# A 31-tap convolution divided anew between GpSimd, ScalarE and VectorE

## The chip, the cores and the metric

The kernel runs on one core of a Trainium2 chip. The metric is the time on the device in microseconds (us) of one execution; a version is given by the median of several runs, and the profile is one further look at one execution, whose own length is called its span.

## The reference

The program is one mixing block with an MLP and then one attention block with a gated MLP, for one sequence of 256 positions and a width of 2048, all in fp32. Only the front of the first block touches the change:

```python
u = rms_norm(h, mix_pre_gain)
p = einsum("bsd,de->bse", u, w_in)                 # 2048 -> 5120
b_gate, c_gate, v_a, val_b, gate_b = split(p, 5 parts of 1024)
y_a = b_gate * causal_dwconv(c_gate * v_a, conv_a_w)         # 3 taps
g = val_b * sigmoid(gate_b)
g = causal_dwconv(g, conv_b_w) + conv_b_bias                 # 31 taps
y_b = silu(layer_norm(g, ln_b_gain, ln_b_bias))
o = einsum("bse,ed->bsd", concatenate([y_a, y_b]), w_out)
# causal_dwconv: out[t, c] = sum_k w[k, c] * u[t - (K - 1) + k, c]
```

So each of 1024 channels is convolved on its own over the 256 positions, with 31 weights of its own.

## The kernel before, in words

**The weights stream.** Every large product reads its weights in slots of 128x1024 fp32 (512 KB). SyncE loads slot g into a ring of four buffers `raw` as soon as VectorE has finished slot g-4 (`load`, L271 to L277). ScalarE copies it to the rounded `w_hi` (`ticks`, L665 to L676) once the load has landed and TensorE has used slot g-4; VectorE writes the rest, `w_lo = raw - w_hi` (`tick`, L972 to L977). TensorE then runs 12 matmuls on the slot (`slots`, L382 to L403): for each of two k tiles and two token tiles one with `w_lo` (L399) and two with `w_hi` (L400, L401). Eight slots make one unit, a product of 256 tokens with 512 columns. ScalarE and VectorE work four slots (`RING`) ahead of TensorE.

**The units of the input product.** `IN_COLS` (L68) orders ten units, 0 to 9. Units 0 and 1 give the first four channel tiles (of 128 channels) of `g`, units 2 and 3 the other four. After an odd unit u of 1, 3, 5, 7 ScalarE evacuates it (L743), VectorE multiplies value and gate into `zz` (L1081), TensorE transposes `zz` once it has done two slots of the next unit (`in_product`, L449 to L457; `turn`, L405 to L418), and ScalarE copies the transposed tiles to `gT` (after units 1 and 3) or to `cvT` (after 5 and 7) (L749 to L753). Only behind these copies, in ScalarE's program order, stand its next slots. Each of these copies adds one to the semaphore `took`. The input of the 31 taps is `gT`, 8 tiles of 128 channels by 30 + 256 positions.

**The taps.** Tile c of the result is `convb[:, c, :]`, 128x256. Six of the eight tiles are computed on VectorE (`taps_long`, L1023 to L1039): the first tap is a multiplication with the bias added (`tap_first`, L259 to L262), each later one a multiply-and-add into `convb` (L1035), 186 instructions in all. They are a generator, from which VectorE's loop takes three after a slot and four after every fourth (L1061), from unit 2 on; what is left is taken in unit 9 at its sixth slot (L1049 to L1051). Each waits, by the semaphore `conv`, for the instruction on the same tile three earlier. The two tiles of `POOL_TILES`, 3 and 7, are computed by GpSimd (L1409 to L1425): per later tap a product into `prod` (L1419) and an add (L1423), 122 instructions. After that GpSimd computes the 3-tap sums of `y_a` from `cvT`, in two halves of four tiles (L1429 to L1445): 24 multiplications of 128x256 and 4 adds of 128x1024 (L1444). VectorE multiplies them by the gate in `yt` (L1097), after units 8 and 9.

**What follows.** TensorE does slots 0 to 4 of unit 9, waits for all the taps (L471, L472) and forms the mean over channels (L474); VectorE subtracts it (L1045); ScalarE squares (L734); TensorE sums the squares (L481), and so on to `y_b`.

ScalarE's share of the stage is in its loop over units (L727 to L761): the copies to `w_hi`, then the evacuation. It has no part in the taps.

```python
1061                        for _ in range(3 + (s % 4 == 3)):
1062                            next(long_, None)
```

Of the kernel before, what the change touches and what calls it, by code (L numbers as in the profile page):

```python
# [24 lines left out]
P = 128  # L25
# [14 lines left out]
POOL_TILES = (3, 7)  # L40
POOL_STEPS = 2 * K_B - 1
# [34 lines left out]
def build_program(nc, t):  # L76
    ctx = ExitStack()
    with ctx:
# [3 lines left out]
        def at(name, kb, shape, dt=F32):  # L82
            return nc.alloc_sbuf_tensor_at(name, shape, dt, offset=base + int(kb * 1024))
# [4 lines left out]
        def sem(name):  # L88
            return ctx.enter_context(nc.semaphore(name))
# [25 lines left out]
        yb = at("yb", 153.5, [P, CT, S])  # L115
        qkT = at("qkT", 144, [P, 2 * NH, S])
# [73 lines left out]
        conv_pool = sem("conv_pool")  # L190
# [190 lines left out]
        def _(pe):  # L381
# [89 lines left out]
            pe.wait_ge(conv, K_B * (CT - len(POOL_TILES)))  # L471
            pe.wait_ge(conv_pool, POOL_STEPS * len(POOL_TILES))  # L472
# [191 lines left out]
        def _(act):  # L664
# [61 lines left out]

            for u in range(10):  # L727
                if u < 9:
                    ticks(G_IN + u * SPU, RING if u else SPU, RING + SPU)
                else:  # L730
                    ticks(G_IN + u * SPU, RING, RING + 5)
# [239 lines left out]
        def _(dve):  # L971
# [51 lines left out]
            def taps_long():  # L1023
                n = 0
                for half_ in range(2):
                    for k in range(K_B):
                        for c in range(4 * half_, 4 * half_ + 3):
                            if k == 0 and c % 4 == 0:
                                dve.wait_ge(took, 4 * half_ // 2 + 2)
                            if k:  # L1030
                                dve.wait_ge(conv, n - 2)
                            if k == 0:
                                tap_first(nc.vector, c).then_inc(conv, 1)
                            else:
                                nc.vector.scalar_tensor_tensor(convb[:, c, :], gT[:, c, k:k + S],  # L1035
                                                               tap_weight(c, k), convb[:, c, :],
                                                               ALU.mult, ALU.add).then_inc(conv, 1)
                            n += 1
                            yield  # L1039
# [7 lines left out]
            for u in range(10):  # L1047
                for s in range(0 if u else RING, SPU):
# [11 lines left out]
                    if u >= 2:  # L1060
                        for _ in range(3 + (s % 4 == 3)):  # L1061
                            next(long_, None)
# [314 lines left out]
        def _(pool):  # L1377
# [30 lines left out]

            for i, c in enumerate(POOL_TILES):  # L1409
                pool.wait_ge(took, 2 * i + 2)  # L1410
                done = i * POOL_STEPS
                if i:
                    pool.wait_ge(conv_pool, done)
                tap_first(nc.gpsimd, c).then_inc(conv_pool, 1)
                for k in range(1, K_B + 1):
                    if k < K_B:
                        if k > 4:
                            pool.wait_ge(conv_pool, done + 2 * k - 6)
                        nc.gpsimd.tensor_scalar(prod[:, k % 4], gT[:, c, k:k + S], tap_weight(c, k),  # L1419
                                                None, ALU.mult).then_inc(conv_pool, 1)  # L1420
                    if k > 1:
                        pool.wait_ge(conv_pool, done + 2 * k - 2)
                        nc.gpsimd.tensor_tensor(convb[:, c, :], convb[:, c, :],  # L1423
                                                prod[:, (k - 1) % 4], ALU.add
                                                ).then_inc(conv_pool, 1)  # L1425

            pool.wait_ge(line_out, 16 * (SKEWS + 1))
            pool.wait_ge(conv_pool, 2 * POOL_STEPS)
# [96 lines left out]
```

## Time and profile before

| | us |
|---|---|
| median of 3 runs | 2596.45 |
| lowest, highest | 2594.0, 2601.71 |
| span of the profiled execution | 2592.5 |
| TensorE busy in it | 2533.8 |
| VectorE busy | 1472.3 |
| ScalarE busy | 1235.2 |
| GpSimd busy | 245.4 |

The page gives the profiled execution no time besides its span, so the span stands for it; it is 3.95 us under the median. A matmul's recorded busy time overlaps its neighbours', so a busy TensorE is not TensorE at its peak. In the views of the trace L followed by a number is a line of the kernel, "xN" the number of instructions that a row holds, and a duration of merged instructions runs from the start of the first to the end of the last. In a row of the order of time, square brackets hold how long the engine was idle ahead of the row, and what ended that. GpSimd is called POOL, VectorE DVE, ScalarE ACT and TensorE PE. The stage of the change lies between 68 us, when the first `gT` is there, and 272 us, when TensorE begins the mean.

### The profile page before, as it was taken

Reading aid. Unit: us, or ns where it says so; the run is one execution under the profiler, and the core shown is the slowest. Engines: PE = TensorE matmul, PEld = TensorE weight load, DVE = VectorE, ACT = ScalarE, POOL = GpSimd, SP = SyncE. Lnnn points to the kernel's source line nnn. Section 1 sums busy time; section 2 is a strip of 40 time slices with the busy share of each in tenths; the row PEclk is TensorE's granted clock in tenths of the full one; section 3 lists DMA queues with packets and bytes.
Section 4 is the critical chain, followed back from the end, with each engine's and each line's share of the span. In section 5 each row is a group of like instructions: output and inputs, shape, how many; then the busy total and the mean of one; then the engine's idle time right before and its main releaser. Section 6 shows DMA issues by size and latency. Waiting matters only on the chain.

```text
span 2592.5 us, 31914 instructions
## 1 busy us (share of the span) xinstructions
PE 2533.8 (98%) x11389; PEld 2096.6 (81%) x11389; DVE 1472.3 (57%) x1548; ACT 1235.2 (48%) x1509; POOL 245.4 (9%) x199
## 2 busy tenths in 40 slices
PE   8888999999999999989999999999999999999999
PEld 7676778888888888878888888888888888888887
DVE  5899655555545555565566655545545544554554
ACT  5333555444444444454465544444544444444443
POOL 0899200000000000001100000000000000000000
PEclk9999999999999999999999999999999999999999
DMA  7554555565566565545555466665565566565654
GB/s 240 185 153 146 162 171 187 188 194 177 195 189 194 189 190 186 192 145 177 187 188 176 155 203 189 192 194 187 179 195 187 192 193 193 179 198 194 191 188 162
DMA packets 247772, 478.36 MB, mean 185 GB/s; under 512 B 16448, under 2 KB 17016, under 8 KB 247388
## 3 DMA queue, kind: packets, MB, share of 16 engines
q1 hardware_dynamic: 244460, 470.14, 56.8%
q0 software_dynamic: 3152, 6.46, 0.7%
q8 instruction: 85, 1.39, 0.2%
q14 instruction: 43, 0.35, 0.0%
q10 hardware_dynamic: 32, 0.01, 0.0%
HBM read 474.42 MB, written 4.47 MB: 185 GB/s over the span
## 4 chain that ended last, share of the span: by engine, by line
PE 91%; DVE 7%; ACT 1%; DMA 1%; issue 0%; POOL 0%; SPq 0%; ACTq 0%; DVEq 0%
PE acc L399 29%; PE acc L401 29%; PE acc L400 29%; DVE convb L1035 4%; DVE w_lo L976 3%; PE tp L416 2%; DMA raw<-w_in_dram 0%; ACT w_hi L676 0%; PE po L593 0%; DMA h<-x_dram 0%; PE sc L563 0%; DVE h L1147 0%; PE tp L581 0%; PE sc L474 0%; PE po L595 0%
## 5 line engine op out<-in xcount | busy, mean ns | idle before, releaser
L976 DVE TENSOR_TENSOR w_lo<-raw,w_hi 128x1024 fp32r<-128x1024 f32 x888 | 1084.5, 1234 | 927.5 <-ACT w_hi L676 924.0
L676 ACT ACTIVATE w_hi<-raw 128x1024 fp32r<-128x1024 f32 x888 | 930.9, 1060 | 1029.2 <-PE acc L401 960.3
L399 PE MATMUL acc<-w_lo,a_hi 128*128 128x512 f32 x2304 | 910.6, 395 | 11.3 <-DVE w_lo L976 10.6
L400 PE MATMUL acc<-w_hi,a_hi 128*128 128x512 f32 x2304 | 901.1, 391 | 0.0
L401 PE MATMUL acc<-w_hi,a_lo 128*128 128x512 f32 x2304 | 901.1, 391 | 0.0
L399 PEld LDWEIGHTS acc<-w_lo,a_hi 128*128 128x128 f32 x2304 | 435.3, 189 | 109.2 <-DVE w_lo L976 14.7
L401 PEld LDWEIGHTS acc<-w_hi,a_lo 128*128 128x128 f32 x2304 | 434.8, 189 | 91.5
L400 PEld LDWEIGHTS acc<-w_hi,a_hi 128*128 128x128 f32 x2304 | 435.3, 189 | 87.4
L399 PE MATMUL acc<-w_lo,b_hi 128*128 128x512 f32 x1120 | 437.2, 390 | 0.4 <-DVE b_lo L1103 0.4
L401 PE MATMUL acc<-w_hi,b_lo 128*128 128x512 f32 x1120 | 436.3, 390 | 0.0
L400 PE MATMUL acc<-w_hi,b_hi 128*128 128x512 f32 x1120 | 436.3, 390 | 0.0
L399 PEld LDWEIGHTS acc<-w_lo,b_hi 128*128 128x128 f32 x1120 | 210.4, 188 | 44.1 <-DVE b_lo L1103 0.8
L401 PEld LDWEIGHTS acc<-w_hi,b_lo 128*128 128x128 f32 x1120 | 210.4, 188 | 43.5
L400 PEld LDWEIGHTS acc<-w_hi,b_hi 128*128 128x128 f32 x1120 | 210.4, 188 | 43.3
L1391 POOL TENSOR_TENSOR rs<-ms,half 128x2 f32<-128x2 f32 x6 | 4.2, 702 | 1240.2 <-DVE ms L1006 1240.2
L1035 DVE SCALAR_TENSOR_TENSOR convb<-gT,cols,convb 128x256 f32<-128x256 f32 x180 | 114.3, 688 | 0.0
L1419 POOL TENSOR_SCALAR prod<-gT,cols 128x256 f32<-128x256 f32 x60 | 99.4, 1657 | 0.0
L990 DVE TENSOR_TENSOR b_lo<-tp,b_hi 128x512 fp32r<-128x512 f32 x54 | 34.8, 686 | 77.3 <-ACT b_hi L695 77.3
L695 ACT ACTIVATE b_hi<-tp 128x512 fp32r<-128x512 f32 x54 | 29.3, 595 | 98.1 <-PE tp L416 98.1
L686 ACT ACTIVATE ev<-acc,rs 128x512 f32<-128x512 f32 x112 | 69.9, 675 | 0.0
L416 PE MATMUL tp<-ident,zz 128*128 128x128 f32 x344 | 47.4, 283 | 19.6 <-DVE zz L1081 19.6
L416 PEld LDWEIGHTS tp<-ident,zz 128*128 128x128 f32 x344 | 42.0, 146 | 26.1 <-DVE zz L1081 20.8
(155 smaller groups left out, 1007.4 us busy)
## 6 DMA issues: line engine op xcount, KB each, us to landing
raw<-w_in_dram SPq DMA_DIRECT2D x272, 512.0 KB, 3.8
raw<-w_down_dram SPq DMA_DIRECT2D x216, 512.0 KB, 4.7
raw<-w_gu_dram SPq DMA_DIRECT2D x176, 512.0 KB, 4.4
raw<-w_up_dram SPq DMA_DIRECT2D x128, 512.0 KB, 3.7
raw<-w_out_dram SPq DMA_DIRECT2D x64, 512.0 KB, 4.4
raw<-w_branch_dram SPq DMA_DIRECT2D x32, 512.0 KB, 3.6
skew_dram<-line_dram POOLq DMA_DIRECT2D x3, 768.0 KB, 14.1
h<-x_dram SPq DMA_DIRECT2D x4, 512.0 KB, 7.8
```

Of the source, the lines that this page charges most:

```text
L399: nc.tensor.matmul(out, xh, wl, start=s == 0 and k == 0, stop=False)
L400: nc.tensor.matmul(out, xh, wh, start=False, stop=False)
L401: mm = nc.tensor.matmul(out, xl, wh, start=False, stop=s == n - 1 and k == KS - 1)
L416: tr = nc.tensor.transpose(tp[:, g, (2 * k + tk) * P:(2 * k + tk + 1) * P], src[:, tk, c:c + P], ident[:, :])
L676: nc.scalar.activation(w_hi[:, ring], raw[:, ring], ACT.Copy).then_inc(hi_ready, 1)
L686: a_ = nc.scalar.activation(dst[:, tk], acc[:, pair, tk], func, scale=rs[:, n, tk:tk + 1])
L695: nc.scalar.activation(dst[:, bass.ds(k0 + 2 * g, 2), :].rearrange("p k s -> p (k s)"), tp[:, g, :], ACT.Copy).then_inc(split_hi, 1)
L976: nc.vector.tensor_tensor(w_lo[:, ring], raw[:, ring], w_hi[:, ring].bitcast(F32), ALU.subtract).then_inc(lo_ready, 1)
L990: nc.vector.tensor_tensor(lo_, tp[:, g, :], hi_.bitcast(F32), ALU.subtract).then_inc(split_lo, 1)
L1035: nc.vector.scalar_tensor_tensor(convb[:, c, :], gT[:, c, k:k + S], tap_weight(c, k), convb[:, c, :], ALU.mult, ALU.add).then_inc(conv, 1)
L1391: nc.gpsimd.tensor_tensor(rs[:, n, :], ms[:, n, :], half[:, :], ALU.pow).then_inc(rs_ok, 1)
L1419: nc.gpsimd.tensor_scalar(prod[:, k % 4], gT[:, c, k:k + S], tap_weight(c, k), None, ALU.mult).then_inc(conv_pool, 1)
```

## The change

GpSimd takes no part in the 31 taps and goes straight from its transfers to the 3-tap sums. The taps are arranged by tap and half (four tiles) instead of by tile. Of each half the taps k = 0, 3, 6, ... 30 (eleven) stay on VectorE tile by tile, with the instructions of before; for the other twenty ScalarE multiplies `gT` by the weights, four instructions of 128x256 into one of four new buffers `scaled`, and VectorE adds the buffer to the four tiles of `convb` in one instruction of 128x1024. `LONG_OPS` is VectorE's list, 128 instructions; `SCALED` has the 40 (half, tap) pairs of ScalarE, 160 instructions. ScalarE takes three of these after each slot of units 2 to 8 and what is left ahead of unit 9; VectorE takes two of its own after a slot, and three after every fourth. ScalarE waits before a buffer's reuse until VectorE has added its last content; VectorE waits before an add for the buffer (`conv_scaled`) and for its own instruction just before. The four buffers lie in parts of `b_hi` and `b_lo` that are written only later, for `y_b`.

```diff
--- before.py
+++ after.py
@@ -37,8 +37,12 @@
 D_A = D // 2
 K_A, K_B = 3, 31
 CT = D_A // P
-POOL_TILES = (3, 7)
-POOL_STEPS = 2 * K_B - 1
+LONG_OPS = tuple((half, k, q)
+                 for half in range(2) for k in range(K_B)
+                 for q in (range(4) if k % 3 == 0 else (None,)))
+SCALED = tuple((half, k) for half, k, q in LONG_OPS if q is None)
+SCALED_AT = tuple(n for n, op in enumerate(LONG_OPS) if op[2] is None)
+BUFS = 4
 FF1 = 4 * D
 FF2 = 5632
 NH = 16
@@ -113,6 +117,8 @@
         convb = at("convb", 162, [P, CT, S])
         dg = at("dg", 170, [P, TT, P])
         yb = at("yb", 153.5, [P, CT, S])
+        scaled = [at("scaled0", 88, [P, 4, S]), at("scaled1", 92, [P, 4, S]),
+                  at("scaled2", 104, [P, 4, S]), at("scaled3", 108, [P, 4, S])]
         qkT = at("qkT", 144, [P, 2 * NH, S])
         m_hi = at("m_hi", 144, [P, KT, S], F32R)
         m_lo = at("m_lo", 160, [P, KT, S], F32R)
@@ -187,7 +193,7 @@
         h_ready = sem("h_ready")
         step0 = sem("step0")
         conv = sem("conv")
-        conv_pool = sem("conv_pool")
+        conv_scaled = sem("conv_scaled")
         conv3 = sem("conv3")
         ya = sem("ya")
         ln_pe = sem("ln_pe")
@@ -468,8 +474,7 @@
             last_in(0, 2)
             in_product(9)
             last_in(2, 5)
-            pe.wait_ge(conv, K_B * (CT - len(POOL_TILES)))
-            pe.wait_ge(conv_pool, POOL_STEPS * len(POOL_TILES))
+            pe.wait_ge(conv, len(LONG_OPS))
             for c in range(CT):
                 mm = nc.tensor.matmul(sc[:, 0:S], mean_w[:, :], convb[:, c, :], start=c == 0,
                                       stop=c == CT - 1)
@@ -724,10 +729,33 @@
                 squares(0, c, h[:, :, c], 2 * c)
 
 
+            def scale_taps():
+
+                for i, (half_, k) in enumerate(SCALED):
+                    act.wait_ge(took, 2 * half_ + 2)
+                    if i >= BUFS:
+                        act.wait_ge(conv, SCALED_AT[i - BUFS] + 1)
+                    for q in range(4):
+                        c = 4 * half_ + q
+                        a_ = nc.scalar.activation(scaled[i % BUFS][:, q, :], gT[:, c, k:k + S],
+                                                  ACT.Copy, scale=tap_weight(c, k))
+                        if q == 3:
+                            a_.then_inc(conv_scaled, 1)
+                        yield
+
+            taps = scale_taps()
+
             for u in range(10):
-                if u < 9:
+                if u < 2:
                     ticks(G_IN + u * SPU, RING if u else SPU, RING + SPU)
+                elif u < 9:
+                    for s in range(SPU):
+                        ticks(G_IN + u * SPU, RING + s, RING + s + 1)
+                        for _ in range(3):
+                            next(taps, None)
                 else:
+                    for _ in taps:
+                        pass
                     ticks(G_IN + u * SPU, RING, RING + 5)
                     for half_ in range(2):
                         act.wait_ge(ln_dve, half_ + 1)
@@ -1021,22 +1049,27 @@
 
 
             def taps_long():
-                n = 0
-                for half_ in range(2):
-                    for k in range(K_B):
-                        for c in range(4 * half_, 4 * half_ + 3):
-                            if k == 0 and c % 4 == 0:
-                                dve.wait_ge(took, 4 * half_ // 2 + 2)
-                            if k:
-                                dve.wait_ge(conv, n - 2)
-                            if k == 0:
-                                tap_first(nc.vector, c).then_inc(conv, 1)
-                            else:
-                                nc.vector.scalar_tensor_tensor(convb[:, c, :], gT[:, c, k:k + S],
-                                                               tap_weight(c, k), convb[:, c, :],
-                                                               ALU.mult, ALU.add).then_inc(conv, 1)
-                            n += 1
-                            yield
+
+                for n, (half_, k, q) in enumerate(LONG_OPS):
+                    if k == 0 and q == 0:
+                        dve.wait_ge(took, 2 * half_ + 2)
+                    if q is None:
+                        i = SCALED_AT.index(n)
+                        dve.wait_ge(conv, n)
+                        dve.wait_ge(conv_scaled, i + 1)
+                        part = convb[:, 4 * half_:4 * half_ + 4, :]
+                        nc.vector.tensor_tensor(part, part, scaled[i % BUFS][:, :, :], ALU.add
+                                                ).then_inc(conv, 1)
+                    else:
+                        c = 4 * half_ + q
+                        if k == 0:
+                            tap_first(nc.vector, c).then_inc(conv, 1)
+                        else:
+                            dve.wait_ge(conv, n - q)
+                            nc.vector.scalar_tensor_tensor(convb[:, c, :], gT[:, c, k:k + S],
+                                                           tap_weight(c, k), convb[:, c, :],
+                                                           ALU.mult, ALU.add).then_inc(conv, 1)
+                    yield
 
             long_ = taps_long()
 
@@ -1058,7 +1091,7 @@
                                                 ).then_inc(ln_dve, 1)
                     tick(G_IN + u * SPU, RING + s)
                     if u >= 2:
-                        for _ in range(3 + (s % 4 == 3)):
+                        for _ in range(2 + (s % 4 == 3)):
                             next(long_, None)
                 if u == 0:
 
@@ -1406,26 +1439,7 @@
                            ).then_inc(gain1_in, 16)
 
 
-            for i, c in enumerate(POOL_TILES):
-                pool.wait_ge(took, 2 * i + 2)
-                done = i * POOL_STEPS
-                if i:
-                    pool.wait_ge(conv_pool, done)
-                tap_first(nc.gpsimd, c).then_inc(conv_pool, 1)
-                for k in range(1, K_B + 1):
-                    if k < K_B:
-                        if k > 4:
-                            pool.wait_ge(conv_pool, done + 2 * k - 6)
-                        nc.gpsimd.tensor_scalar(prod[:, k % 4], gT[:, c, k:k + S], tap_weight(c, k),
-                                                None, ALU.mult).then_inc(conv_pool, 1)
-                    if k > 1:
-                        pool.wait_ge(conv_pool, done + 2 * k - 2)
-                        nc.gpsimd.tensor_tensor(convb[:, c, :], convb[:, c, :],
-                                                prod[:, (k - 1) % 4], ALU.add
-                                                ).then_inc(conv_pool, 1)
-
             pool.wait_ge(line_out, 16 * (SKEWS + 1))
-            pool.wait_ge(conv_pool, 2 * POOL_STEPS)
             for half_ in range(2):
                 pool.wait_ge(took, 4 + 2 * half_ + 2)
                 sums = conva[:, 4 * half_:4 * half_ + 4, :]
```

## Rows read from the trace of the kernel before

**Rows 1.** Page: busy time by engine; shares of the chain by line

```profile
PE 2533.8 (98%) x11389; PEld 2096.6 (81%) x11389; DVE 1472.3 (57%) x1548; ACT 1235.2 (48%) x1509; POOL 245.4 (9%) x199
PE acc L399 29%; PE acc L401 29%; PE acc L400 29%; DVE convb L1035 4%; DVE w_lo L976 3%; PE tp L416 2%; DMA raw<-w_in_dram 0%; ACT w_hi L676 0%; PE po L593 0%; DMA h<-x_dram 0%; PE sc L563 0%; DVE h L1147 0%; PE tp L581 0%; PE sc L474 0%; PE po L595 0%
```

**Rows 2.** Stretches: busy us (x) PE, PEld, DVE, ACT, POOL; clock; DMA; GB/s

```profile
90.00:120.00 30.00, 21.72 (x89) 15.87 (x87) 29.39 (x40) 9.65 (x10) 30.00 (x24) 0.95 0.54 168
330.00:360.00 30.00, 30.00 (x134) 24.86 (x133) 14.62 (x12) 13.88 (x17) 0.00 (x0) 1.00 0.59 194
```

**Rows 3.** Chain of waits in order of time: start us, us, what

```profile
80.52 11.45 DMA raw<-w_in_dram
...
118.87 1.14 DVE zz L1081
120.06 1.98 PE tp L416 x8
...
174.76 1.15 DVE zz L1081
...
231.69 1.15 DVE zz L1081
...
271.90 3.72 PE sc L474 x16
```

**Rows 4.** Who waited for whom, 92 to 272 us: in total, times, longest

```profile
PE tp L416 <- DVE zz L1081: 19.6, 3, 6.7
PE acc L399 <- DVE w_lo L976: 9.9, 13, 2.9
```

**Rows 5.** VectorE in order of time: start, us, instruction, idle before

```profile
34.12 0.16 DVE L1004 TENSOR_REDUCE ms<-ssq 128x2 f32<-128x8 f32 x1 [3.48 <-ACT junk L709]
34.32 0.17 DVE L1006 TENSOR_SCALAR ms<-ms 128x2 f32<-128x2 f32 x1
...
71.53 1.27 DVE L1035 SCALAR_TENSOR_TENSOR convb<-gT,cols,convb 128x256 f32<-128x256 f32 x3
...
93.09 1.35 DVE L976 TENSOR_TENSOR w_lo<-raw,w_hi 128x1024 fp32r<-128x1024 f32 x1 [0.61 <-ACT w_hi L676]
...
127.82 1.89 DVE L1035 SCALAR_TENSOR_TENSOR convb<-gT,cols,convb 128x256 f32<-128x256 f32 x3
...
236.46 1.42 DVE L976 TENSOR_TENSOR w_lo<-raw,w_hi 128x1024 fp32r<-128x1024 f32 x1 [3.64 <-ACT w_hi L676]
...
249.97 3.41 DVE L976 TENSOR_TENSOR w_lo<-raw,w_hi 128x1024 fp32r<-128x1024 f32 x1
...
258.84 1.71 DVE L1035 SCALAR_TENSOR_TENSOR convb<-gT,cols,convb 128x256 f32<-128x256 f32 x3
...
261.61 2.11 DVE L1035 SCALAR_TENSOR_TENSOR convb<-gT,cols,convb 128x256 f32<-128x256 f32 x4
263.64 1.27 DVE L1097 TENSOR_TENSOR yt<-tp,conva 128x512 f32<-128x512 f32 x2
...
267.05 1.41 DVE L976 TENSOR_TENSOR w_lo<-raw,w_hi 128x1024 fp32r<-128x1024 f32 x1
```

**Rows 6.** VectorE group with the new add's shape, whole run

```profile
L1187 DVE TENSOR_TENSOR wide<-wide,ev 128x1024 f32<-128x1024 f32 x16 | 19.5, 1219 | 0.3 <-ACT ev L683 0.3
```

**Rows 7.** ScalarE in order of time

```profile
122.56 2.00 ACT L676 ACTIVATE w_hi<-raw 128x1024 fp32r<-128x1024 f32 x2
...
131.36 1.06 ACT L676 ACTIVATE w_hi<-raw 128x1024 fp32r<-128x1024 f32 x1 [1.66 <-PE acc L401]
...
140.49 1.25 ACT L686 ACTIVATE ev<-acc,rs 128x512 f32<-128x512 f32 x2
...
298.27 1.09 ACT L768 ACTIVATE yb<-convb,cols 128x256 f32<-128x256 f32 x2
```

**Rows 8.** GpSimd in order of time: the three-tap sums, first and last

```profile
231.57 4.67 POOL L1439 TENSOR_SCALAR conva<-cvT,cols 128x256 f32<-128x256 f32 x4 [0.16 <-issue]
...
272.11 3.09 POOL L1444 TENSOR_TENSOR conva<-conva,prod 128x1024 f32<-128x1024 f32 x1
```

## The prediction

> **What bounds the kernel now.** I read the page first: TensorE is busy for 98% of the span and holds nearly all of the chain that ended last, but VectorE's tap line L1035 has 4% of that chain, some 100 us, and only this stage has those taps [rows 1]. The stretches come next: with its work undisturbed TensorE has 134 matmul records in 30 us, and between 90 and 120 us only 89, while VectorE is busy for 29.4 of 30 [rows 2]. So VectorE bounds the stage. The chain in order of time shows how. It holds one slow load up to 92.0 us, then almost only VectorE up to a product `zz` (ends at 120.0; the first of three here), the transposes, and VectorE again to the second `zz` (ends at 175.9) and the third (232.8), until TensorE starts the mean at 271.9 [rows 3]. TensorE's waits agree: 19.6 us for the three `zz` and 9.9 us for `w_lo` [rows 4].
>
> One round from `zz` to `zz` is 16 slots and took 55.9 and 56.9 us. TensorE's own pace is 2.72 us a slot (1.66 idle + 1.06, where ScalarE follows TensorE [rows 7]), so its round is 43.5 plus 2.0 for the transposes, 45.5.
>
> **The new price of VectorE's work.** A tap took 1.89 us for three, pitch 0.60 once the overlap of 0.08 is taken off, while GpSimd worked on the taps; the same three took 1.27, pitch 0.40, at 71.5 us, before GpSimd had begun [rows 5]. Beside GpSimd's 3-tap sums it is 1.71 for three, pitch 0.54 [rows 5]. The new add has the shape of L1187, 1.219 us, pitch 1.14 [rows 6]. GpSimd's 122 instructions go, and with them the 0.20 a tap. The new list is 88 single taps at 0.40 (35.2) and 40 adds at 1.14 (45.6), 80.8 us. Of these, 40 adds and 20 first-of-four taps wait for the instruction just before. Nearest row: a multiplication that waits for its predecessor starts at 34.32, 0.04 after that one's end at 34.28, where an unwaiting one would start 0.08 before the end [rows 5]; so 0.12 each. A slot's subtraction stands between in almost half the cases, so 35 of them, 4.2 us. Sum 85.0 over 128, or 0.66 each; bounds 0.63 (no such wait) and 0.78 (a tap stays at 0.60).
>
> The Trainium skill, "VectorE: DVE Perf Modes", section "The DRAIN you can't avoid", has the next operation start only when the pipe is empty, semaphore or not, so that these waits would cost nothing. The rows show an overlap of 0.08 that a wait would lose, so here they disagree; by that rule 4.2 us less would be spent in the whole list.
>
> **The sum, stretch by stretch.**
>
> First, up to 92 us the loads govern: one took 11.45 us [rows 3]. GpSimd's transfers that compete with it are not moved, and VectorE had only 0.61 us idle before 93.09 [rows 5]; I take no gain here (bounds 0 and 2).
>
> Second, 93.1 to the first `zz`: 8 subtractions at 1.14 (9.1), 18 list entries at 0.66 (12.0; before, 26), `zz` 1.14: it ends at 115.3 instead of 120.0, gain 4.7.
>
> Third, the round to 175.9: idle after `zz` 3.64, as the row at 236.46 shows for this pattern [rows 5], 16 subtractions 18.2, 36 entries 23.9, `zz` 1.14, together 46.9 against 55.9: gain 9.0. TensorE's 45.5 lies just under it.
>
> Fourth, the round to 232.8. GpSimd now starts the 3-tap sums when the second `zz` has been transposed and copied, not at 231.57 [rows 8], so half of them falls in here. What they cost VectorE: from 236.46 to 263.64 it did 8 subtractions and 26 taps in 27.2 us, which at 1.14 and 0.40 would be 9.1 + 10.4 = 19.5, so 7.7 more: 0.14 on each tap (3.6), and about 4 for subtractions or taps held behind GpSimd's large adds, as the subtraction of 3.41 us at 249.97 beside the usual 1.21 [rows 5]. With 11 taps instead of 26 that is 6.2. The round is 53.1 against 56.9: gain 3.8.
>
> Fifth, unit 8, where the second half of the 3-tap sums runs (from the third `zz` on) as before: 9.1 + 12.0 + 6.2 = 27.3 against 27.2: gain 0.
>
> Sixth, unit 9: `w_lo` for slot 4 is ready at 268.5 [rows 5], TensorE needs 2.72, so 271.2; the mean waited until 271.9 for the last taps [rows 3]. With two entries left instead of four or more, the wait goes: gain 0.7. What is late next is slot 4 itself, behind `yt` and its roundings. GpSimd's last add, which held VectorE up to 277.3 (3.09 us from 272.11 [rows 8]), ends earlier; this lies under TensorE's two slots of 5.4 us, and I give it nothing.
>
> **ScalarE.** The 160 multiplications are hidden only while its round fits. From `zz` to its first copy to `w_hi` 2.55 us (120.01 to 122.56); 16 copies at pitch 0.94 (2.00 for two) 15.2; two evacuations of 1.25, 2.4; `zz` 1.15; and 48 multiplications of x. That is 21.3 + 48x. The price x is not in the trace. The nearest row is a 128x256 activation out of SBUF with a column as scale and one as bias, 1.09 us for two, pitch 0.49 [rows 7]; with one column I take 0.45 (bounds 0.38, under which nothing of this length falls, and 1.06, the whole 128x1024 copy). The round is 42.9, hidden under VectorE's 46.9 by 4 us. By order, the entry that VectorE needs in a slot has been produced in the same slot of ScalarE or earlier, up to three earlier in the second half, and ScalarE's wait for a free buffer is for an entry one to five slots back, so neither waits in steady state. A late ScalarE would hold back `w_hi`, for which VectorE and then TensorE wait. SyncE's loads wait for `w_lo`; at TensorE's pace 194 GB/s flow without a wait [rows 2].
>
> In all 4.7 + 9.0 + 3.8 + 0 + 0.7 = 18.2 us. The sum is made against the span of 2592.5, giving 2574.3; the median shown is 3.95 above that span, and the predicted median is 2596.45 - 18.2 = 2578.2. About 0.3%, 8 us, is what a measurement of this kernel can tell from no change.
>
> **Rivals.**
>
> (a) *TensorE becomes the bound* (0.20). If the 3-tap sums no longer hurt VectorE and its own waits cost nothing, rounds fall to 45.5. Then the gains are 5.3, 10.4, 11.4, and in unit 9 up to 5.7 (eleven slots, 29.9, and transposes, 1.5, after 234.8 make 266.2 instead of 271.9): 32.8, or 2563.7. For it: TensorE's round is only 1.4 us below VectorE's. Against: the 3-tap sums visibly stretch VectorE [rows 5].
>
> (b) *GpSimd holds up the long adds* (0.12). The Trainium skill, "SBUF — State Buffer", section "Who interferes with whom", has VectorE and GpSimd share a port pair as an exclusive lock, held for a whole instruction by whoever starts first, whenever VectorE has two inputs in SBUF and GpSimd reads there. As a mechanism of this kernel: in each of the two halves of the 3-tap sums some 5.6 adds run, and each waits for one GpSimd multiplication of 1.2 us (4.67 us for four [rows 8]). That costs 6.7 twice, 18.2 - 13.4 = 4.8 us gained, 2591.6. Against: subtractions of the same shape were mostly at 1.21 beside GpSimd [rows 5].
>
> (c) *ScalarE becomes the bound, and the kernel is slower* (0.06). It decides at x = 0.53, where 21.3 + 48x reaches 46.9, and makes the round longer than before from x = 0.72. At 0.85, in the upper half of my bounds (each multiplication stopping at its wait for the buffer), the rounds are 62.1, 6.2 and 5.2 longer, the first stretch 2.5 and unit 8 2: 16 slower, 2612. Against: 0.85 is nearly the pitch of a 128x1024 copy, for a quarter of its elements.
>
> (d) *The change doesn't free VectorE*: GpSimd leaves, but a tap stays at 0.60, so something else had stretched it. At 0.78 an entry the rounds are 51.1; gains 2.5, 4.8 and 5.8 (no stretch added), 13 in all; it lies within my range and I count it with the forecast.
>
> **Chances and range.** Forecast (gain 10 to 26) 0.62, (a) 0.20, (b) 0.12, (c) 0.06. Low 2562 takes in (a); high 2592 takes in (b)'s centre and the bad ends of the prices. Faster by over 0.3% is 0.62 less 0.02, plus 0.20, plus a quarter of (b): 0.83. Within 0.3%: 0.11, mostly (b). Slower: 0.06.
>
> **What would show it.** Right: taps at 0.40 pitch up to the second `zz`; adds at 1.22 us; a `zz` round of about 47 us and then 53; multiplications on ScalarE of about 0.5 us; TensorE's wait for `zz` down from 6.5 us to 1 or 2 each; VectorE still leading the chain. Wrong: ScalarE's `w_hi` as releaser of long VectorE idle times ((c)); adds above 1.5 us after 165 us ((b)); TensorE alone in the chain there ((a)); or a first `zz` that does not come earlier than 120 us, which would mean that the loads govern beyond 93 us.

## The result, and the profile after

The changed kernel takes 2575.35 us (median of four runs, 2574.43 to 2577.28) against 2596.93 for the kernel before (now also four runs); the ratio is 0.9914 with a 95% interval of 0.9891 to 0.9937, so 16 to 28 us faster. The span of its profiled execution is 2574.3 us, 18.2 less than the 2592.5 of before.

The page of the changed kernel, engines and shares of the chain by line, beside [rows 1]. L1061 is the new add, L1069 the single tap, L740 the multiplication on ScalarE:

```profile
PE 2531.6 (98%) x11389; PEld 2097.8 (81%) x11389; DVE 1444.6 (56%) x1490; ACT 1296.4 (50%) x1669; POOL 101.9 (4%) x77
...
PE acc L405 30%; PE acc L407 30%; PE acc L406 30%; PE tp L422 2%; DVE w_lo L1004 1%; DVE convb L1061 1%; DVE convb L1069 1%; DMA raw<-w_in_dram 0%; ACT w_hi L681 0%; ACT scaled L740 0%; PE po L598 0%; PE sc L568 0%; DMA h<-x_dram 0%; DVE h L1180 0%; PE tp L586 0%
```

VectorE's taps had 4% of the chain; the two tap lines now have 2% together, and TensorE's three matmul lines have gone from 29% to 30% each. GpSimd's busy time is down by 143 us, ScalarE's up by 61. Two stretches of the changed kernel, to be held against [rows 2]:

```profile
90.00:120.00 30.00, 24.26 (x102) 19.63 (x101) 25.00 (x30) 21.44 (x40) 0.00 (x0) 0.89 0.55 165
120.00:150.00 30.00, 30.00 (x134) 24.83 (x133) 29.53 (x38) 27.07 (x49) 0.00 (x0) 1.00 0.66 193
248.00:252.80 4.80, 4.51 (x13) 3.60 (x14) 4.43 (x6) 1.33 (x2) 0.00 (x0) 0.66 0.50 154
```

TensorE has 102 records between 90 and 120 us where it had 89, and 134, its full number, in the next 30; the third row is read further down. VectorE in order of time, to be held against [rows 3, 5] (start us, us, instruction, idle before):

```profile
73.16 2.48 DVE L1061 TENSOR_TENSOR convb<-convb,scaled 128x1024 f32<-128x1024 f32 x2
...
76.70 1.27 DVE L1069 SCALAR_TENSOR_TENSOR convb<-gT,cols,convb 128x256 f32<-128x256 f32 x3
...
114.33 1.22 DVE L1114 TENSOR_TENSOR zz<-ev 128x1024 f32<-128x1024 f32 x1
119.18 1.23 DVE L1004 TENSOR_TENSOR w_lo<-raw,w_hi 128x1024 fp32r<-128x1024 f32 x1 [3.63 <-ACT w_hi L681]
...
161.18 1.22 DVE L1114 TENSOR_TENSOR zz<-ev 128x1024 f32<-128x1024 f32 x1
...
179.47 2.52 DVE L1069 SCALAR_TENSOR_TENSOR convb<-gT,cols,convb 128x256 f32<-128x256 f32 x1
...
190.40 3.40 DVE L1004 TENSOR_TENSOR w_lo<-raw,w_hi 128x1024 fp32r<-128x1024 f32 x1
...
213.85 1.22 DVE L1114 TENSOR_TENSOR zz<-ev 128x1024 f32<-128x1024 f32 x1
...
243.60 1.28 DVE L1130 TENSOR_TENSOR yt<-tp,conva 128x512 f32<-128x512 f32 x2
```

and the end of the stage in the chain that ended last:

```profile
252.75 3.61 PE sc L479 x16
```

The chain counts the mean from the end of the matmul before it; its first matmul starts at 252.55, 189.1 us after the `zz` that follows unit 1, and this is the figure to which the runs below are held. Three taps in a row took 1.27 us, and two adds 2.48, each 1.23, 0.02 apart. The `zz` start at 114.33, 161.18 and 213.85. GpSimd's 3-tap sums have moved forward, into the third round (from 164.5 us; their second half begins at 217.61). Each of the two long adds there holds up one VectorE instruction: beside the add at 178.89 a single tap takes 2.52 us, beside the one at 190.34 a subtraction takes 3.40:

```profile
164.49 6.29 POOL L1453 TENSOR_SCALAR conva<-cvT,cols 128x256 f32<-128x256 f32 x4 [90.15 <-ACT cvT L779]
...
178.89 2.81 POOL L1458 TENSOR_TENSOR conva<-conva,prod 128x1024 f32<-128x1024 f32 x1
...
190.34 2.38 POOL L1458 TENSOR_TENSOR conva<-conva,prod 128x1024 f32<-128x1024 f32 x1
```

**Where the time went.** All from the start of the `zz` after unit 1, which is at 64.00 before and 63.46 after:

| stretch | before | after | gain | predicted |
|---|---|---|---|---|
| to the first `zz` of the stage | 54.79 | 50.87 | 3.9 | 4.7 |
| second round | 55.90 | 46.85 | 9.1 | 9.0 |
| third round | 56.92 | 52.67 | 4.3 | 3.8 |
| third `zz` to `yt` (unit 8) | 32.03 | 29.75 | 2.3 | 0 |
| `yt` to the mean (unit 9) | 8.26 | 9.15 | -0.9 | 0.7 |
| sum | 207.90 | 189.29 | 18.6 | 18.2 |

**Which engine sets each round.** The second round is no longer VectorE's. TensorE's transposes after the three `zz`, with its idle time before them:

```profile
115.60 1.97 PE L422 MATMUL tp<-ident,zz 128*128 128x128 f32 x8 [5.08 <-DVE zz L1114]
...
162.45 1.09 PE L422 MATMUL tp<-ident,zz 128*128 128x128 f32 x8 [0.22 <-DVE zz L1114]
...
215.12 1.75 PE L422 MATMUL tp<-ident,zz 128*128 128x128 f32 x8 [3.01 <-DVE zz L1114]
```

Between the first two rows TensorE is idle for those 0.22 us and nothing more, so its own work fills the round: 1.6 us until the first matmul of the slots, 16 slots of 2.72 (43.5), and about 1.3 us because the first matmuls run at a low granted clock (0.50 from 114 to 117 us, 0.53 from 117 to 120), start to start 0.43 us instead of 0.23. From 115.6 to 154.2 us the chain that ended last consists of TensorE's matmuls alone. ScalarE waits 0.46 us for TensorE before a copy to `w_hi`, and near the end VectorE waits for that copy:

```profile
154.17 1.06 ACT L681 ACTIVATE w_hi<-raw 128x1024 fp32r<-128x1024 f32 x1 [0.46 <-PE acc L407]
```

```profile
155.26 1.23 DVE L1004 TENSOR_TENSOR w_lo<-raw,w_hi 128x1024 fp32r<-128x1024 f32 x1 [0.85 <-ACT w_hi L681]
```

Without that wait VectorE's round would be about 46.0 us, so the two engines are within 1 us of each other. From 92.6 us to the first `zz`, in the third round and in unit 8 VectorE is behind, as TensorE's waits of 5.08 and 3.01 us show.

### The profile page after: what moved, and what is told of

Same layout as the page of the kernel before. It is cut to its first block, busy times and chain, and to the rows that moved or that the text cites. A ratio compares the mean times of both kernels' runs of the same rounds, so it can differ in the third digit from the quotient of the medians.

```text
span 2574.3 us, 31968 instructions
## 1 busy us (share of the span) xinstructions
PE 2531.6 (98%) x11389; PEld 2097.8 (81%) x11389; DVE 1444.6 (56%) x1490; ACT 1296.4 (50%) x1669; POOL 101.9 (4%) x77
## 4 chain that ended last, share of the span: by engine, by line
PE 93%; DVE 4%; issue 1%; ACT 1%; DMA 1%; POOL 0%; ACTq 0%; SPq 0%; DVEq 0%
PE acc L405 30%; PE acc L407 30%; PE acc L406 30%; PE tp L422 2%; DVE w_lo L1004 1%; DVE convb L1061 1%; DVE convb L1069 1%; DMA raw<-w_in_dram 0%; ACT w_hi L681 0%; ACT scaled L740 0%; PE po L598 0%; PE sc L568 0%; DMA h<-x_dram 0%; DVE h L1180 0%; PE tp L586 0%
## 5 line engine op out<-in xcount | busy, mean ns | idle before, releaser
L740 ACT ACTIVATE scaled<-gT,cols 128x256 f32<-128x256 f32 x160 | 69.5, 497 | 8.3 <-DVE convb L1061 8.3
L688 ACT ACTIVATE ev<-acc 128x1024 f32<-128x1024 f32 x48 | 48.5, 1011 | 13.2 <-PE acc L407 13.2
```

The costliest lines, as they stand in the source:

```text
L688: nc.scalar.activation(dst, acc[:, pair], func).then_inc(evacuated, 1)
L740: a_ = nc.scalar.activation(scaled[i % BUFS][:, q, :], gT[:, c, k:k + S], ACT.Copy, scale=tap_weight(c, k))
```

## The experiments

Each ratio below is against runs of the kernel before on the same chip, whose median was 2595.0 to 2596.0 in these series. It is formed from the runs and not from the two medians, from whose quotient it differs by up to 0.002. The changed kernel was not run again in these series: where a run is set against it by a few us, the two come from different chips, the intervals of the ratios overlap, and the trace has to show the difference.

**One half of the change: GpSimd leaves, VectorE does all.** `all_vector` takes the taps from GpSimd and gives none to ScalarE:

```diff
-                 for q in (range(4) if k % 3 == 0 else (None,)))
+                 for q in range(4))
...
-                        for _ in range(2 + (s % 4 == 3)):
+                        for _ in range(4 + s % 2):
                             next(long_, None)
```

> GpSimd leaves the 31 taps, but ScalarE does not step in: VectorE computes all 248 of them one tile at a time. Theory (a tap costs VectorE 0.40 us once GpSimd is silent, and 0.54 to 0.60 beside it): a round from zz to zz is 3.6 idle + 18.2 subtractions + 72 taps at 0.40 (28.8) + about 1.2 for taps that wait for their predecessor + 1.1 = 53 us, against 55.9 before; the round and the unit with the 3-tap sums are longer than before (about 62 and 33 us). In all some 5 us slower than the kernel before, about 2602 us. Rival (taps stay at 0.60 whatever GpSimd does): a round of 67 us and 2635 us or more. Rival (the long adds are what brings the gain, GpSimd's silence nothing): the same as that.

Measured: 2594.93 us, ratio 0.9994 (0.9981 to 1.0006): no change. VectorE's group of taps from 70 to 265 us, and its `zz` in order of time:

```profile
L1069 DVE SCALAR_TENSOR_TENSOR convb<-gT,cols,convb 128x256 f32<-128x256 f32 x240 | 112.1, 514 | 1.7
```

```profile
118.66 1.22 DVE L1114 TENSOR_TENSOR zz<-ev 128x1024 f32<-128x1024 f32 x1
...
171.53 1.22 DVE L1114 TENSOR_TENSOR zz<-ev 128x1024 f32<-128x1024 f32 x1
...
231.29 1.22 DVE L1114 TENSOR_TENSOR zz<-ev 128x1024 f32<-128x1024 f32 x1
```

The second round is 52.9 us, as expected, with taps of 0.514 against 0.689 in the same stretch of the kernel before. The third is 59.8 instead of 62, so the 3-tap sums cost it 6.9, not 9. So GpSimd's silence pays for the 62 taps that VectorE took over, and for nothing more. The expected loss of 5 us did not come: up to the mean the stage is only 1 us longer than in the kernel before.

**The other half: ScalarE and the grouped adds help, GpSimd stays.** `keep_pool` has the new division for six tiles, and GpSimd's loop of before for the other two:

```diff
-                 for q in (range(4) if k % 3 == 0 else (None,)))
+                 for q in (range(3) if k % 3 == 0 else (None,)))
...
+            for i, c in enumerate(POOL_TILES):
...
-                        part = convb[:, 4 * half_:4 * half_ + 4, :]
+                        part = convb[:, 4 * half_:4 * half_ + 3, :]
```

> ScalarE and the grouped adds help with six tiles (120 multiplications, 40 adds of 128x768), and GpSimd keeps its two tiles as before. Theory: VectorE's list is 66 single taps at 0.60 and 40 adds of about 0.99, 78 us in all against 85 in the changed kernel, so the rounds are about 46 us; but GpSimd ends its taps only at about 227 us, and the first half of the 3-tap sums at about 250, for which yt waits: GpSimd becomes the bound, and the mean starts at about 260 us instead of 252.8. About 2582 us, 7 slower than the changed kernel. Rival (GpSimd beside VectorE costs more than it computes): rounds of 50 us and more, adds above 1.2 us. Rival (keeping GpSimd is free, and only VectorE's list counts): 2572.

Measured: 2598.97 us, ratio 1.0002 (0.9987 to 1.0016): no change either, where a gain was expected. GpSimd's adds and the new adds of VectorE by group (68 to 290 us), and the wait of `yt`:

```profile
L1460 POOL TENSOR_TENSOR convb<-convb,prod 128x256 f32<-128x256 f32 x60 | 67.1, 1119 | 0.2
...
L1065 DVE TENSOR_TENSOR convb<-convb,scaled 128x768 f32<-128x768 f32 x40 | 47.8, 1196 | 3.0 <-ACT scaled L744 2.4
```

```profile
123.05 1.74 DVE L1118 TENSOR_TENSOR zz<-ev 128x1024 f32<-128x1024 f32 x1
...
180.27 1.21 DVE L1118 TENSOR_TENSOR zz<-ev 128x1024 f32<-128x1024 f32 x1
...
233.47 1.21 DVE L1118 TENSOR_TENSOR zz<-ev 128x1024 f32<-128x1024 f32 x1
...
267.00 1.29 DVE L1134 TENSOR_TENSOR yt<-tp,conva 128x512 f32<-128x512 f32 x2 [9.46 <-POOL conva L1481]
```

The rounds are 57.2 and 53.2 us, not 46, as the first rival said. An add of 768 elements takes 1.196 us on average, nearly as long as one of 1024 beside an idle GpSimd (1.223), and GpSimd's own adds have gone from 0.956 to 1.119. The average hides two cases: up to 170 us most of these adds take 1.40 us or more, from 176 to 235 us most take 0.95, though GpSimd works throughout; why was not tried. The theory's other half held too: GpSimd ends its taps at 242.5 us, and `yt` waits 9.5 us for the 3-tap sums. I had priced the long adds at 0.99 beside GpSimd. Each half of the change is worth nothing alone, and both together 21 us.

**GpSimd's old instructions put back, for nothing.** `pool_busy` is the changed kernel with the loop of before on GpSimd, its sum going to a spare tile:

```diff
+            for i, c in enumerate((3, 7)):
+                pool.wait_ge(took, 2 * i + 2)
...
+                        nc.gpsimd.tensor_tensor(spare[:, :], spare[:, :],
+                                                prod[:, (k - 1) % 4], ALU.add
```

> The changed kernel, with GpSimd given its 122 former instructions back, their result going to a spare tile that nobody reads. Theory (GpSimd's instructions stretch VectorE's): single taps go from 0.40 to 0.60 pitch, the second round from 46.9 to 51 or 52 us; the 3-tap sums start only at about 225 us, so yt waits for them up to about 250 us. 2588 us, 13 slower than the changed kernel. Rival (the lock holds every long add for a GpSimd instruction too): adds of 1.8 us or more, a second round of 58 us and 2600 or more. Rival (GpSimd's silence is worth nothing): 2575.

Measured: 2610.22 us, ratio 1.0062 (1.0041 to 1.0084), 35 us over the changed kernel where 13 were expected. VectorE by group in about one round, first in `pool_busy` (125 to 178 us), then in the changed kernel (117 to 162 us):

```profile
L1006 DVE TENSOR_TENSOR w_lo<-raw,w_hi 128x1024 fp32r<-128x1024 f32 x16 | 23.2, 1450 | 3.6 <-ACT w_hi L683 3.6
L1071 DVE SCALAR_TENSOR_TENSOR convb<-gT,cols,convb 128x256 f32<-128x256 f32 x22 | 14.2, 681 | 0.1
L1063 DVE TENSOR_TENSOR convb<-convb,scaled 128x1024 f32<-128x1024 f32 x10 | 13.6, 1356 | 0.2
```

```profile
L1004 DVE TENSOR_TENSOR w_lo<-raw,w_hi 128x1024 fp32r<-128x1024 f32 x16 | 19.6, 1222 | 4.7 <-ACT w_hi L681 4.5
L1061 DVE TENSOR_TENSOR convb<-convb,scaled 128x1024 f32<-128x1024 f32 x10 | 12.2, 1223 | 0.2
L1069 DVE SCALAR_TENSOR_TENSOR convb<-gT,cols,convb 128x256 f32<-128x256 f32 x22 | 9.7, 481 | 0.1
```

The single taps grew by 0.200 us, as the theory said (22 of them, 4.4 us). What it had left out are the subtractions, by 0.228 (16, 3.6 us), and the adds, by 0.133 (10, 1.3 us): the round is 55.5 us instead of 46.85, 8.6 more and not 4.4. The first stretch and the third round are longer by 7.2 and 6.0 us, and the way from the third `zz` to `yt` by 14.3; that holds a wait of 12.15 us for GpSimd, itself late:

```profile
280.07 1.29 DVE L1132 TENSOR_TENSOR yt<-tp,conva 128x512 f32<-128x512 f32 x2 [12.15 <-POOL conva L1482]
```

So both my theory (taps only) and its first rival (every add held, 1.8 us) were off: taps, subtractions and adds, which all read two operands in SBUF, are all stretched, by 0.13 to 0.23 us on average.

**The 3-tap sums left out.** In `no_three` GpSimd fills their tile with ones:

```diff
-                for k in range(K_A):
...
+                for q in range(2 * K_A - 1):
+                    v = nc.gpsimd.memset(sums[:, :, 52 * q:min(52 * q + 52, S)], 1.0)
+                    v.then_inc(conv3, 1)
```

> The changed kernel with GpSimd's 3-tap sums left out (their tile is filled with ones instead, so y_a is not computed). Theory (the 3-tap sums stretch VectorE by about 6 us in each of two stretches): the third round is 47 us instead of 52.7, unit 8 drops from 25.1 to 21 us or less, and TensorE becomes the bound there; the mean starts about 10 us earlier, 2565 us. Rival (they run beside VectorE and cost nothing on the path): 2575.

Measured: 2564.27 us, ratio 0.9882 (0.9864 to 0.9900).

```profile
161.49 1.22 DVE L1114 TENSOR_TENSOR zz<-ev 128x1024 f32<-128x1024 f32 x1
...
208.33 1.22 DVE L1114 TENSOR_TENSOR zz<-ev 128x1024 f32<-128x1024 f32 x1
...
234.68 1.28 DVE L1130 TENSOR_TENSOR yt<-tp,conva 128x512 f32<-128x512 f32 x2
```

The third round is 46.8 us instead of 52.7, and from the third `zz` to `yt` it is 26.4 instead of 29.8. In both stretches VectorE's only idle time, with the sums or without, is the one after `zz`, so the sums cost it 5.8 us in the third round (I had taken 6.2) and 3.4 in unit 8. The difference is in the long adds: of the two in each half one holds up a tap by 2 us in either stretch, and the other a subtraction by 2.2 in the third round only; in unit 8 it starts at 243.54 us, as `yt` begins.

**ScalarE's room.** `double_scale` does each multiplication twice:

```diff
+                        nc.scalar.activation(twin[i % BUFS][:, q, :], gT[:, c, k:k + S],
+                                             ACT.Copy, scale=tap_weight(c, k))
```

> The changed kernel with each of the 160 multiplications done twice on ScalarE (the second into a spare tile). Theory (ScalarE's round is 21.3 + 48x, decides at x = 0.53 and loses against the kernel before from x = 0.72; the twins make x = 0.80): rounds of 60 us, 27 us slower than the changed kernel, 2602 us, and slower than the kernel before. Rival (ScalarE has room beside TensorE's pace): under 2585 us.

Measured: 2608.01 us, ratio 1.0032 (1.0015 to 1.0049), slower than the kernel before, and 33 us over the changed kernel instead of 27.

```profile
123.74 1.22 DVE L1118 TENSOR_TENSOR zz<-ev 128x1024 f32<-128x1024 f32 x1
...
183.49 1.23 DVE L1118 TENSOR_TENSOR zz<-ev 128x1024 f32<-128x1024 f32 x1 [0.27 <-ACT ev L693]
...
243.23 1.23 DVE L1118 TENSOR_TENSOR zz<-ev 128x1024 f32<-128x1024 f32 x1 [0.26 <-ACT ev L693]
```

Rounds of 59.75 and 59.74 us: 21.3 + 48 x 0.80 is 59.7, and the second and third `zz` wait for ScalarE's evacuation. The formula of rival (c) holds; what was not in the expectation are 8.6 us more in the first stretch and 4.3 in unit 8. In the changed kernel three multiplications take 1.29 us, pitch 0.40:

```profile
78.33 1.29 ACT L740 ACTIVATE scaled<-gT,cols 128x256 f32<-128x256 f32 x3
...
196.96 0.51 ACT L740 ACTIVATE scaled<-gT,cols 128x256 f32<-128x256 f32 x1 [4.67 <-DVE convb L1061]
```

so ScalarE's work in a round is 21.3 + 19.2 = 40.5 us there, 6.3 under the round's 46.85. The last row is a wait of 4.67 us for a free buffer, which I had said would not occur in steady state; it begins at 192.3, while VectorE is held behind GpSimd's long add (190.40 to 193.80). `bufs6` asks whether it costs:

```diff
-BUFS = 4
+BUFS = 6
```

> The changed kernel with six buffers scaled instead of four. Theory: ScalarE's 8.3 us of waits for a buffer go, but VectorE was not waiting for what they delayed: 2575 us, within 1 us. Rival (the waits for a buffer in the third round, one of 4.7 us, hold back w_hi): 2 to 4 us faster.

Measured: 2574.99 us, ratio 0.9897 (0.9850 to 0.9943). The interval is too wide to tell 2 to 4 us from none; the trace shows no gain: the mean begins 188.9 us after the `zz` of unit 1, and 189.1 in the changed kernel.

**The idle time after `zz`.** `hoist` moves one of ScalarE's copies to `w_hi` ahead of its copies to `gT` and `cvT`; `hoist2` moves two (`hoist_bufs6` is `hoist` with six buffers):

```diff
-                        ticks(G_IN + u * SPU, RING + s, RING + s + 1)
+                        if s or u % 2:
+                            ticks(G_IN + u * SPU, RING + s, RING + s + 1)
...
                     i = u // 2
...
+                    ticks(G_IN + (u + 1) * SPU, RING, RING + 1)
```

> The changed kernel, with ScalarE copying the next slot to w_hi ahead of its copies to gT and cvT instead of behind them (four times). Theory (VectorE bounds the rounds, and its 3 to 3.6 us of idle time after each zz are on the path): the idle time after zz goes, and each round shortens until TensorE's 45.5 us bind: 1.4 in the second round, 3.6 in the third, about 3 in unit 8. 8 us faster than the changed kernel, 2567 us. Rival (ScalarE or TensorE sets the rounds): 2575. Rival (the copies to gT and cvT come 1 us later and delay the taps and the 3-tap sums): 2576 to 2578.

> The earlier copy to w_hi and six buffers together. Theory: the idle time after zz is what costs, and once it is gone the third round is set by VectorE beside the 3-tap sums: 2567 us, as with the earlier copy alone. Rival (with the idle time gone, ScalarE's waits for a buffer begin to bind): 2 us or more faster than the earlier copy alone.

> The changed kernel with two of ScalarE's copies to w_hi, not one, ahead of its copies to gT and cvT. With one, VectorE's idle time had only moved behind the next slot (2.9 us). Theory (the rounds are VectorE's, until TensorE's 45.5 us bind): with two slots of work in hand, 5 us, VectorE has no idle time of over 1 us after a zz; rounds of about 45.5 and 49 us, the mean 2 to 3 us earlier than with one, 2567 to 2568 us. Rival (TensorE bound already with one copy ahead): 2570, as with one.

Measured: 2570.33 (ratio 0.9909, 0.9889 to 0.9928), 2570.89 (0.9885, 0.9849 to 0.9920) and 2568.26 us (0.9898, 0.9882 to 0.9915). The medians are 5, 4 and 7 us under the changed kernel's; in the traces the mean begins 184.8, 184.9 and 181.8 us after the `zz` of unit 1 instead of 189.1. First `hoist`, then `hoist2`, after the first `zz`:

```profile
119.72 1.23 DVE L1006 TENSOR_TENSOR w_lo<-raw,w_hi 128x1024 fp32r<-128x1024 f32 x1 [2.90 <-ACT w_hi L681]
```

```profile
112.31 1.22 DVE L1116 TENSOR_TENSOR zz<-ev 128x1024 f32<-128x1024 f32 x1
...
121.14 1.23 DVE L1006 TENSOR_TENSOR w_lo<-raw,w_hi 128x1024 fp32r<-128x1024 f32 x1 [3.76 <-ACT w_hi L681]
...
159.42 1.22 DVE L1116 TENSOR_TENSOR zz<-ev 128x1024 f32<-128x1024 f32 x1
...
209.66 1.22 DVE L1116 TENSOR_TENSOR zz<-ev 128x1024 f32<-128x1024 f32 x1
```

In the second round the idle time was not removed but moved, behind one slot (2.9 us) and behind two (3.76), and the round did not get shorter: 47.2 us in `hoist`, 47.1 in `hoist2`, 46.85 in the changed kernel. The rival held there: TensorE sets this round, as in the changed kernel, and waits 0.22 us for its second `zz` in both runs, so VectorE waits for `w_hi` wherever its list is shorter than TensorE's. With two copies ahead, ScalarE's third needs a ring buffer that TensorE frees only after the transposes and one more slot, and TensorE runs most of that slot with its matmuls 0.43 us apart instead of 0.23 (granted clock 0.50 from 112 to 117 us). The gain lies where VectorE is the later engine, in the third round (51.6 and 50.2 instead of 52.7), in unit 8, and in 1 us or more ahead of the first `zz`.

**The second half of the sums later.** `late_sums` and, with two copies ahead, `hoist2_late`:

```diff
                 pool.wait_ge(took, 4 + 2 * half_ + 2)
+                if half_:
+                    pool.wait_ge(conv, 126)
```

> The changed kernel with GpSimd's second half of the 3-tap sums started only when VectorE has done 126 of its 128 entries. Theory (beside these sums VectorE is stretched by about 4 us in unit 8, and TensorE leaves some room there): yt after unit 8 comes 3 to 4 us earlier, the mean at about 249.5 instead of 252.8; the second half is done at about 265, ahead of its use at 271: 2572 us, 3 faster. Rival (TensorE sets unit 8): 2575. Rival (the sums end too late for the second yt): 2577 or more.

> Both together: two copies ahead, and the second half of the 3-tap sums late. Theory: the third round stays stretched by the first half of the sums (about 49 us), the rest is TensorE's; 2565 us. Rival (the two gains are the same room, TensorE's): no faster than the two copies alone.

Measured: 2572.91 (ratio 0.9910, 0.9894 to 0.9927) and 2565.24 us (0.9883, 0.9867 to 0.9900). The rows are from `late_sums`:

```profile
214.03 1.22 DVE L1114 TENSOR_TENSOR zz<-ev 128x1024 f32<-128x1024 f32 x1
...
240.29 1.29 DVE L1130 TENSOR_TENSOR yt<-tp,conva 128x512 f32<-128x512 f32 x2
...
272.40 1.28 DVE L1130 TENSOR_TENSOR yt<-tp,conva 128x512 f32<-128x512 f32 x2
```

Unit 8 is 26.3 us from `zz` to `yt` instead of 29.8, as without the sums, and the second `yt`, at 272.4, does not wait for GpSimd. Against the kernel before, the ratio of `late_sums` is hardly below the changed kernel's 0.9914, so its gain rests on the trace: the mean begins 4.4 us earlier and the second `yt` 3.0. `hoist2_late` has the mean 7.2 us earlier and the second `yt` 9.0; its span is 9.6 us below the changed kernel's and its median 10, 1 over `no_three`, which does less work. Each measured against the kernel before on its own chip, the medians give 8 us (29.7 against 21.6).

## Why the prediction was right

Measured 2575.35 against a forecast of 2578.2 and a range of 2562 to 2592; the span, which the sum was made for, is 2574.3, as forecast. The bulk of the mechanism is right, the price of VectorE's list; that the span agrees to 0.1 us is luck, since several terms were off and cancel. Point by point:

- *VectorE bounds the stage, and the second round goes to 46.9.* The round is 46.85, but the step is only in part right, and the agreement is luck: in this round TensorE binds, not VectorE. TensorE's round was put at 45.5, without the low clock of its first matmuls after a wait, and is 46.6; VectorE's own was put at 46.9 and would be about 46.0. The sign named for it, a wait of TensorE of 1 or 2 us for each `zz`, did not come: the waits are 5.08, 0.22 and 3.01 us (8.3 in all, where the kernel before had 19.6). The stretch before it and the two after it are VectorE's, as said.
- *The new price of VectorE's work.* Right, one by one: a tap 0.40, an add 1.14 and 0.11 more where it waits for its predecessor (2.48 us for two, against 2.36 for two subtractions without such a wait at 21.9 us of the trace before). The pieces that carry it are a quiet GpSimd (`pool_busy`) and ScalarE's share (`all_vector`).
- *GpSimd leaving takes 0.20 off each tap, and only that.* Half right. The 0.20 is confirmed, but the subtractions of the weights stream gain too, from 1.282 us on average in the second round of before to 1.222. I had read 1.21 us in most rows and overlooked the longer ones (1.75 and more) in a sum where the mean was what counted. It did not show in the total, because I summed the new rounds from undisturbed prices.
- *No gain up to 92 us, 4.7 to the first `zz`.* 3.9. The loads governed as said: the idle time ahead of the subtraction at 92.60 is 0.90 us.
- *The third round at 53.1.* 52.7, and the surcharge for the 3-tap sums was 5.8 where 6.2 was taken. The parts named for it, 0.14 on each of 11 taps and about 4 for instructions held behind long adds, add up to 5.6, not 6.2. The 4 is confirmed: one tap and one subtraction were held, by 2.0 and 2.2 us.
- *Unit 8 gains nothing.* Wrong: 2.3 us. The failing term is the surcharge of 6.2, which measured 3.4 there: `no_three` takes 26.4 from `zz` to `yt`, the changed kernel 29.8. The last long add of the half no longer falls on VectorE's list ahead of `yt`.
- *Unit 9 gains 0.7.* Wrong: it lost 0.9. I had slot 4 at TensorE's usual 2.72 us; it took over 4.2, at a lower clock (last section). The errors of units 8 and 9 cancel but for 0.7.
- *The price x of a multiplication, 0.45.* It is 0.40, with 0.497 for one, so ScalarE had 6 us of room in the second round, not 4, and rival (c) was farther off. The Trainium skill ("ScalarE: Activation LUTs", "What ACT_TABLE_LOAD costs") gives 186 ns + 0.833 ns an element + 93 ns for a column operand, estimated 492 ns here, and an overlap of 93: the trace agrees, with 497 and 0.40. `double_scale` shows its threshold to be real.
- *GpSimd holds up the long adds*, rival (b): its mechanism exists, its size was too high here. In the two stretches of the 3-tap sums (164.5 to 192.8 and 217.6 to 246 us) six adds each take 1.37 us on average, 0.15 more than undisturbed, not a whole GpSimd instruction; the adds above 1.5 us that it named as its sign did not come. The Trainium skill ("SBUF — State Buffer", "Who interferes with whom") has the later one blocked for the whole instruction of the other; that agrees with the 3.40 us at 190.40 beside an add of 2.38 us that began 0.06 us earlier, while beside GpSimd's shorter instructions the mean cost was 0.13 to 0.23 us (`pool_busy`), well under one of them.
- *TensorE becomes the bound*, rival (a): its mechanism is there in the second round, at 46.85 us and not 45.5, but not in the third and not in unit 8, where the 3-tap sums keep VectorE behind; so the gain of 32.8 did not come. `no_three` and `hoist2_late` come within 2 us of the 2563.7 given for it, by shorter third rounds and units 8; their second rounds are 47.4 and 47.0.
- *The change doesn't free VectorE*, (d): excluded, a single tap takes 0.481 us in the second round and a pitch of 0.40.
- *3.95 us between span and median.* Wrong: in all four runs of the changed kernel 1.8 us lie between span and time. The rest lies in the profiled execution of before, itself some 2.6 us under the median of its four runs, while that of the changed kernel lies 0.8 over its own. That is why the medians differ by 21.6 and the spans by 18.2; the interval of the ratio holds both.

## What to carry to other kernels

Two engines that slow each other have to be priced together: taking work off GpSimd freed VectorE of 0.2 us on each short two-operand instruction, and putting it back, with its result unread, cost 35 us, some 12 of them because GpSimd itself was late. A change can be two halves, each worth nothing alone (0.9994 and 1.0002 here) and 0.9914 together, so a failed half is no verdict on the whole. When the bound engine's list is shortened, ask stretch by stretch which engine is last afterwards. An agreement of the time with the forecast does not answer that: here the second round came out as forecast, but set by TensorE, and taking away VectorE's idle time in it gained nothing. In the stretches where VectorE was still behind, its idle time after `zz` and the side work it overlaps gave another 8 to 10 us.

## What the runs showed that was not expected

TensorE lost time to its clock right after being made to wait, but not always. After the wait of 5.08 us for the first `zz` it ran at a granted clock of 0.50 to 0.53 (1.2 GHz being 0.50) from 114 to 120 us, after the wait of 0.22 us at 162.45 at 1.00. In the changed kernel slot 4 of unit 9 begins at 248.29 us after an idle time of 2.3 us, and the stretch from 248 to 252.8 us (third row of the stretches above) has a granted clock of 0.66, a mixture of 2.4 GHz and 1.2 GHz. TensorE in order of time:

```profile
248.63 0.39 PE L406 MATMUL acc<-w_hi,a_hi 128*128 128x512 f32 x1
248.86 0.40 PE L407 MATMUL acc<-w_hi,a_lo 128*128 128x512 f32 x1
...
251.27 0.63 PE L405 MATMUL acc<-w_lo,a_hi 128*128 128x512 f32 x1
251.70 0.63 PE L406 MATMUL acc<-w_hi,a_hi 128*128 128x512 f32 x1
```

Two matmuls start 0.23 us apart at first and 0.43 from 249.6 us on. In the kernel before the same slot follows an idle time of 2.9 us and keeps 0.23 throughout, in a stretch (268 to 272 us) with a clock of 1.00. Why the one wait was followed by the lower clock and the other not is open; no run tried it.
